# A paged-attention decode step: value pages on every fourth partition, groups of four pages from four blocks, page sums over two groups

## What is computed

```python
# DEC_BATCH 8, DEC_SEQ 4, PAST_LEN 2048, PAGE_SIZE 128, N_HEADS 8, HEAD_DIM 64, MOBA_BLOCK 256, MOBA_TOPK 3
k_full = cache_k[layer, page_table[:, :n_full * ppb]]            # 16 pages a sequence, 2 pages a block
k_mean = jnp.mean(k_full.reshape(db, n_full, ppb * PAGE_SIZE, N_HEADS, HEAD_DIM), axis=2)
gate = jnp.einsum('bthd,bnhd->bhtn', q, k_mean)                  # one score a block
_, sel = lax.top_k(gate, n_sel)                                  # the best 3 of 8 blocks
s_sel = jnp.einsum('bthd,bhtkd->bhtk', qf, k_sel) + bias         # scores of the chosen blocks
p = jax.nn.softmax(jnp.concatenate([s_sel, s_loc], axis=-1), axis=-1)
out = jnp.einsum('bhtk,bhtkd->bthd', p[..., :n_k_sel], v_sel) + jnp.einsum('bhtk,bkhd->bthd', p[..., n_k_sel:], v_loc)
```

## Time and profile before

| | us |
|---|---|
| median of 3 runs | 565.19 (561.32 to 569.01) |
| the profiled execution | 564.61 |
| its span | 562.8 |

### The profile page before, as it was taken

The page is one execution under the profiler, slowest core; times in us unless marked ns, Lnnn a source line. Parts: engine busy times, 40 slices in busy tenths (PEclk is TensorE's granted clock), DMA queues, the critical chain, the costliest instruction groups (busy, mean ns, idle before and its releaser), DMA issues.

```text
span 562.8 us, 13854 instructions
## 1 busy us (share of the span) xinstructions
PE 521.1 (93%) x5624; PEld 474.5 (84%) x5624; DVE 305.9 (54%) x710; ACT 179.9 (32%) x389; POOL 121.4 (22%) x108
## 2 busy tenths in 40 slices
PE   8999999999999999999984899799957899999994
PEld 5999999999999999988984789799846799998763
DVE  6623223577755665667642648875412264694524
ACT  6522222243433433544431222221331132233313
POOL 2101211314132123123132143441451100000002
PEclk9999999999999999999998899899988999999998
DMA  8647443686598999994999989999999795351004
GB/s 247 177 151 195 146 128 103 197 221 186 173 261 197 267 273 210 275 270 123 275 237 289 257 211 265 230 262 272 238 255 226 186 259 192 120 190 38 1 9 149
DMA packets 73561, 112.00 MB, mean 199 GB/s; under 512 B 5501, under 2 KB 35338, under 8 KB 73498
## 3 DMA queue, kind: packets, MB, share of 16 engines
q1 hardware_dynamic: 72122, 107.51, 71.8%
q0 software_dynamic: 1232, 3.36, 2.0%
q10 hardware_dynamic: 144, 0.26, 0.1%
HBM read 106.57 MB, written 4.53 MB: 197 GB/s over the span
## 4 chain that ended last, share of the span: by engine, by line
PE 70%; DMA 17%; DVE 6%; SPq 2%; issue 2%; POOL 1%; ACT 1%; POOLq 0%; DVEq 0%; ACTq 0%
PE BK L576 33%; DMA KRAW<-in_cache_k 17%; PE BK L596 9%; PE BK L916 8%; PE BK L731 4%; PE BK L745 4%; PE BK L665 2%; DVE KT L1326 2%; PE BK L793 2%; PE BK L810 2%; PE BK L800 2%; SPq L504 1%; PE BK L846 1%; PE BK L773 1%; DVE XR L1238 1%
## 5 line engine op out<-in xcount | busy, mean ns | idle before, releaser
L576 PE MATMUL BK<-XH,WH 128*128 128x272 f32 x672 | 202.7, 302 | 0.0
L576 PE MATMUL BK<-XH,WL 128*128 128x272 f32 x672 | 194.3, 289 | 0.0
L576 PE MATMUL BK<-XL,WH 128*128 128x272 f32 x672 | 194.3, 289 | 0.0
L1326 DVE STREAM_TRANSPOSE KT<-KRAW 128x512 f32<-128x512 f32 x128 | 88.6, 701 | 90.4 <-DMA KRAW<-in_cache_k 90.1
L576 PEld LDWEIGHTS BK<-XH,WH 128*128 128x128 f32 x672 | 127.6, 190 | 10.9 <-issue 10.2
L576 PEld LDWEIGHTS BK<-XL,WH 128*128 128x128 f32 x672 | 127.5, 190 | 0.0
L576 PEld LDWEIGHTS BK<-XH,WL 128*128 128x128 f32 x672 | 127.2, 189 | 0.0
L1686 POOL TENSOR_TENSOR WL<-WRAW,WH 128x1024 fp32r<-128x1024 f32 x32 | 76.7, 2397 | 217.6 <-ACT WH L965 217.6
L731 PE MATMUL BK<-KT,QW 128*32 128x128 f32 x1024 | 37.2, 289 | 26.5 <-DVE KT L1326 26.5
L965 ACT ACTIVATE WH<-WRAW 128x1024 fp32r<-128x1024 f32 x52 | 54.9, 1056 | 16.6 <-PE BK L596 16.0
L731 PEld LDWEIGHTS BK<-KT,QW 128*32 128x32 f32 x1024 | 27.7, 115 | 32.4 <-DVE KT L1326 28.9
(11 more groups left out here) (207 smaller groups left out, 807.1 us busy)
## 6 DMA issues: line engine op xcount, KB each, us to landing
KRAW<-in_cache_k SPq DMA_DIRECT2D x128, 256.0 KB, 6.4
WRAW<-in_w_in SPq DMA_DIRECT2D x21, 1024.0 KB, 8.6
VRAW<-in_cache_v SPq DMA_DIRECT2D x56, 256.0 KB, 5.5
VQT<-in_cache_v SPq DMA_DIRECT2D x28, 256.0 KB, 6.3
VEX<-in_cache_v SPq DMA_DIRECT2D x24, 256.0 KB, 7.9
VGU<-in_cache_v SPq DMA_DIRECT2D x20, 256.0 KB, 5.4
WO<-in_w_o SPq DMA_DIRECT2D x4, 1024.0 KB, 7.0
XR<-in_x_prompt SPq DMA_DIRECT2D x4, 512.0 KB, 5.6
```

Source lines behind the costliest of these rows:

```text
L576: last = mm(BK[h][:, 0:HALF], w[:, n % 2, k, :], x[:, k, cols], start=(i == 0 and w is WH and x is XA), stop=(i == KC - 1 and w is WL))
L1326: dve.transpose(KT[:, i % KB, :], KRAW[:, i % KR, :]).then_inc(kt_ok, 1)
```

## The change

Three things, which go together. (1) Group q no longer has pages 4q to 4q+3 but every second page from `first_of(q)`: one page of each of four blocks; two groups make four blocks. (2) `KT` holds a group as piece, t, page j: DVE writes with a step of four elements, PE reads 128 adjacent columns, and column 4t+j belongs to page j. So the turned probabilities of page j lie on partitions j, j+4, ..., and its values are loaded there: `VP[place][j:P:4]`, with the same source, the same four runs of 2 KB in each of 32 partitions. (3) Sums and maxima are taken once for two groups, over 256 columns read with a step of four elements. The adding of the mask (`SC`) walks its columns in the new order. Lines of the changed file stand six to seven further down.

```diff
+def first_of(q):
+
+    return 8 * (q // 2) + q % 2
@@
-        KT = sb("KT", [P, KB, DA])
+        KT = sb("KT", [P, KB // 4, 16, 32, 4])
@@ load_k
-                    sp.load(k_regs, PTB[0:1, i:i + 4])
+                    sp.load(k_regs, PTB[0:1, first_of(i // 4):first_of(i // 4) + 7:2])
@@ load_v
-                sp.load(v_regs, PTB[0:1, 4 * q:4 * q + 4])
+                sp.load(v_regs, PTB[0:1, first_of(q):first_of(q) + 7:2])
@@
-                    sp.dma_start(VP[place][32 * j:32 * j + 32], cache_v[0, bass.ds(page, 1)].rearrange("a (b t) h d -> (a t) b (h d)", b=4)
+                    sp.dma_start(VP[place][j:P:4], cache_v[0, bass.ds(page, 1)].rearrange("a (b t) h d -> (a t) b (h d)", b=4)
@@ page_scores
-                        last = mm(SCB[b % 2][32 * c:32 * c + 32, x * P:(x + 1) * P], QW[:, f, :], KT[:, at4:at4 + 4, 32 * f:32 * f + 32],
+                        last = mm(SCB[b % 2][32 * c:32 * c + 32, x * P:(x + 1) * P], QW[:, f, :], KT[:, q % 2, f].rearrange("p t j -> p (t j)"),
@@ page_turn
-                dve.transpose(KT[:, i % KB, :], KRAW[:, i % KR, :]).then_inc(kt_ok, 1)
+                dve.transpose(KT[:, i // 4 % 2, :, :, i % 4], KRAW[:, i % KR, :].rearrange("p (f d) -> p f d", f=16)).then_inc(kt_ok, 1)
@@ page_sums
-                b, x = q // 4, q % 4
+                b, x = q // 4, q % 4 // 2
@@
-                sc = SCB[b % 2][:, x * P:(x + 1) * P].rearrange("p (n k) -> p n k", n=2)
-                summed = dve.tensor_reduce(R[:, 2 * x:2 * x + 2], sc, AX.X, ALU.add)
-                if x == 3:
+                sc = SCB[b % 2][:, 2 * x * P:(2 * x + 2) * P].rearrange("p (k n) -> p n k", n=4)
+                summed = dve.tensor_reduce(R[:, 4 * x:4 * x + 4], sc, AX.X, ALU.add)
+                if x == 1:
                     link(summed)
-                    last_page = SCB[b % 2][:, 4 * P - 32:4 * P]
+                    last_page = SCB[b % 2][:, 3 * P + 3:4 * P:4]
@@
-                peak = dve.tensor_reduce(KP[:, 2 * x:2 * x + 2], sc, AX.X, ALU.max)
+                peak = dve.tensor_reduce(KP[:, 4 * x:4 * x + 4], sc, AX.X, ALU.max)
@@ choose
-                dve.tensor_tensor(SC[:].rearrange("p (n k) -> p n k", n=8), SCB[b % 2][:].rearrange("p (n k) -> p n k", n=8),
-                                  bass.AP(sel.tensor, sel.offset, [list(sel.ap[0]), [1, 8], [0, 64]]), ALU.add).then_inc(eb_ok, 1)
+                dve.tensor_tensor(SC[:].rearrange("p (x k n) -> p x k n", x=2, n=4), SCB[b % 2][:].rearrange("p (x k n) -> p x k n", x=2, n=4),
+                                  bass.AP(sel.tensor, sel.offset, [list(sel.ap[0]), [4, 2], [0, 64], [1, 4]]), ALU.add).then_inc(eb_ok, 1)
@@ DVE program
-                if t % 4 == 1 and 5 <= t < PAGES:
+                if t % 8 == 1 and 9 <= t < PAGES:
                     page_sums(t // 4 - 1)
```

More of the change, by code:

```diff
@@ L726, in page_scores @@
                     wait(pe, pt_ok, b - 1)
-                at4 = 4 * (q % 2)
                 for k in range(4):
```

## The result

| | before | after |
|---|---|---|
| median of 20 runs on the same chip, us | 568.29 (559.22 to 577.25) | 557.02 (551.14 to 562.13) |
| ratio | | 0.9855 [0.9822, 0.9889] |
| the profiled execution, us (its span) | 564.61 (562.8) | 553.3 (551.5) |

Forecast were 28 us; 557.02 lies 1 us outside the range of 526 to 556. The first view to read is the table of engines on the page of after, with two other lines of that page: the DMA queue of SP, and the shares of the chain of work that ended last.

What follows compares the result with a forecast made beforehand. DMA was taken to bound 273 to 448 us, slowed by value pages, and PE 100 to 262 us. From the profiled 564.6 us, 29.9 less DMA time plus 2 for waits gave 537 us, range 526 to 556.

Steps and rivals of the forecast that it cites:

- 29.9 less and 2 back: DMA, 273 to 448 us: 68 value pages at 351 instead of 221 GB/s save 29.9 us; 2 us added for waits.
- the shape of the load: Value loads: low rate comes from 32 rows of four 2 KB runs, not where they land; time 565 us; chance 0.14.
- I take the write of the same step: nothing: DVE's 128 turnings: writing with a 16-byte step adds 0.03 us a page, 4 us in all, counted as nothing.
- The other bound: DVE's turnings: upper bound from a read with 128-byte step, 1.0 ns an element, 0.5 us a page, 64 us.
- a rival of 0.08: DVE becomes the bound at the turnings; gain shrinks from 0.84 us more each, within 307 us; example 625 us; chance 0.08.
- What hides it: DVE's idle time, 87 us from 273 to 448 us and 56 from 100 to 262, covers the longer turnings.
- two signs of being wrong on DVE: Profile after the change, DVE: turnings exceed 1 us and DVE's share passes 80%.
- turnings 0.5 us longer: DVE's turnings: DVE at 264 of 307 us, prompt attention waits, 5 to 15 us of gain lost; 542 to 552 us; chance 0.06.
- Residual waits: PE, 273 to 448 us: single groups wait for key pages behind value groups and weights; 2 us added.
- SP: counted as nothing: SP's issuing: same rows; page numbers read with a step of two remain one load, hidden behind waits; no cost.
- Reductions, mask and PE: DVE reductions 17.2 to 13.2 us (up to 21.4), hidden; mask counted as nothing; PE's scores stay at 273 ns.
- PE alone as the bound: Whole kernel: all other traffic speeds up too, stalls and low clock go; 528 us; chance 0.17.

Runs made afterwards that it cites:

- e7: Kernel before with only the values moved, each page to every second partition of one half (0 to 63 or 64 to 127); 567.22 us, ratio 0.9978.
- e1: Kernel before with only the value pages moved to every fourth partition, reordered when the mask is added in four pieces; 541.18 us, ratio 0.953.
- e3: Changed kernel with turnings writing 512 adjacent elements, keys of a group then in wrong order; 544.15 us, ratio 0.9577.
- e4: Changed kernel with turnings writing every second element (8-byte step), keys of a group in wrong order; 548.17 us, ratio 0.9594.
- e2: Changed kernel with value pages back on 32 neighbouring partitions, mask added in two pieces that restore page order; 577.41 us, ratio 1.0111.

## Why the prediction was wrong

**DMA: right.** Value pages spread over all partitions move at the pace of weight loads when both share the queue (356 to 408 GB/s, the slices shown under e7), and by e1 this is worth 4.7%. In the stretch that DMA bound, e1 needs 160.9 instead of 186.4 us, 25.5 less; the forecast was 29.9 less and 2 back. That the shape of the load was the cause (a rival with 0.14) is refuted by e1, whose loads have the same shape.

**DVE: the step that failed.** It is the sentence "I take the write of the same step: nothing", which left the longer turnings out of the sum. They measured 0.417 us a page, 49 us of DVE time, and some 16 us of the kernel's time (after against e3). The sentence rested on the copy at L1270, 32 elements in 176 ns with a step of 16 bytes, beside 174 ns for another copy of 32. That is nearly all fixed cost. At 0.81 ns an element 32 elements would be 26 ns, and the copy does not show even that; why not is open. The other bound, 0.5 us a page from the strided reading at L1315, was near the measured 0.417 us, and the third line of evidence was a rule of the Trainium skill on lines, which I had made a rival of 0.08. The Trainium skill (SBUF — State Buffer, section "Specifications (TRN2)") says that SBUF has 16-byte lines, that two hits in a line are needed for full bandwidth, and that each cross to a new line pays. The runs agree: two fp32 in a line are free (e4: 702 against 701 ns), one costs 0.81 to 0.88 ns an element (after; e1 beside e7). My reading of it, a turning several times as long, gave too high a price: the fixed part and the reading stay, and 701 ns become 1118.

**What hides it: half wrong.** I set 87 us of DVE's idle time against the turnings' growth. It hid more than half of it, 16 us lost for 49 us of work. But idle time is an average. The last page of a group is turned behind whatever DVE does for the prompt, and each turning also releases the ring place that the next key load waits for: SP waits 102.3 us for turned keys in after and 88.6 in e3. How much each of these ways cost was not measured apart. The chain of after shows a turning right behind such work, and one that ends just as PE's scores begin after 3.11 us of waiting (chain first, then PE's timeline):

```profile
352.33 2.31 DVE VN L1483
354.65 1.02 DVE KT L1332
...
362.95 1.00 DVE KT L1332
...
364.00 1.08 PE L737 MATMUL BK<-KT,QW 128*32 128x128 f32 x32 [3.11 <-DVE KT L1332]
```

The work ahead of the turning, `VN` at L1483, is itself drawn out, as it is in before (2.60 us): its row in DVE's timeline takes 2.39 us, where others take 0.75, and runs beside a piece of POOL's weight work (`WL`, 351.71 to 354.10 us). In after the same befell the rows that multiply `TG` and `G` (L1358). Here is the first of them, from the timelines of DVE and POOL:

```profile
246.45 2.61 DVE L1358 SCALAR_TENSOR_TENSOR G<-TG,G 128x544 f32<-128x544 f32 x1
...
246.10 2.37 POOL L1692 TENSOR_TENSOR WL<-WRAW,WH 128x1024 fp32r<-128x1024 f32 x1 [8.44 <-ACT WH L971]
```

Seven of these eight rows start while POOL makes a `WL` piece and end some 0.6 us after it; six of them take 2.1 to 2.9 us. In before two do, one of them with 2.48 us, and the rows clear of POOL's work take 0.7. Together the eight grew from 7.6 to 17.5 us. E2, with slow turnings too, has 15.8 us and e3 has 8.7, so the longer turnings had shifted DVE's other work against POOL's, a cost that the forecast had not thought of. What it is worth in the kernel's time was not measured apart.

Where PE had no gap, 4.5 us were lost between the first scores and group 15. The forecast had said that 0 to 262 us would keep its length. Of its two signs of being wrong on DVE one came, turnings over 1 us; DVE's share stayed under 80% (126.52 of 162 us, then 118.30). The rival "turnings 0.5 us longer" (0.06; 542 to 552 us, in terms of a profiled execution) had the mechanism and the size; 553.3 is 1 us above it. In the rival that made DVE the bound, the 307 us leave out 262 to 273 us, whose DVE work is counted; with them DVE has 318 us, and turnings could grow by 0.92 instead of 0.84 us.

**Residual waits: too small.** Two us were added for single groups that wait; e1, whose turnings take 698 ns, still waits 11.1 us for `KT` in all. The next point may be one reason; that was not measured apart.

**SP: counted as nothing, wrong.** The issue of a value page takes twice as long once its partitions are stepped. The rows give min, median and max ns from 100 to 450 us (e7's over the whole execution), first of before, then of after, e2 and e7, with the key pages of after last:

```profile
L504 SPq DMA_DIRECT2D VRAW<-in_cache_v x52: 316/318/1128, 156.3 to 429.7; - x52
...
L511 SPq DMA_DIRECT2D VRAW<-in_cache_v x52: 602/603/1452, 162.7 to 423.5; - x52
...
L511 SPq DMA_DIRECT2D VRAW<-in_cache_v x52: 316/329/1247, 165.0 to 440.2; - x52
...
L504 SPq DMA_DIRECT2D VRAW<-in_cache_v x56: 596/597/1222, 47.4 to 428.2; - x56
...
L491 SPq DMA_DIRECT2D KRAW<-in_cache_k x124: 331/338/1732, 106.6 to 426.6; - x124
```

Eight value issues took 3.9 us from the first to the last before. In the chain of after they take 6.5 us, and the first key page behind them is issued 7.5 us after the first value page instead of 4.4; the key page that the chain goes on with is a later one:

```profile
271.88 0.62 SPq L511
272.69 0.60 SPq L511
273.49 0.60 SPq L511
...
278.33 0.86 SPq L511
279.38 0.44 SPq L491
...
281.03 7.72 DMA KRAW<-in_cache_k
```

With 0.79 us from one value page to the next (272.69, 273.49, 274.28) SP offers an estimated 332 GB/s at most. So value pages alone don't fill DMA: from 293 to 297 us, with four value pages issued from 293.23 us on, the rate is 222 GB/s as before, but at a share of 0.71. The rates over 300 GB/s that the forecast wanted to see come in the windows shown where weights and key pages stand in the queue too.

```profile
293.00:297.00 4.00, 4.00 (x34) 4.00 (x33) 4.00 (x8) 1.51 (x3) 0.00 (x0) 1.00 0.71 222
```

This is also in e1, which still gained 4.7%; what it costs there was not measured apart from the rest.

**Reductions, mask and PE: right.** Reductions take 16 x (383 + 425) ns = 12.9 us, forecast 13.2; the mask 682 ns, as before. One run instead of four in the scores' moving operand: still a median of 273 ns. The granted clock after 273 us rose from 0.94 to 0.97, not to 1.00; in e1 it did rise to 1.00, where no stall for `KT` was longer than 2.6 us (8.0 in before, 3.8 in after).

**PE alone as the bound (528 us, 0.17)** was not reached by any kernel; the best, e1, has PE busy for 160.30 of 173 us from 262 us on.

## What to carry to other kernels

Split a layout change by who pays: which engine writes with a step, which reads with one, and which transfers land where; here the DMA half alone gives 4.7% and the compute half takes some 3 points back, and the permutation fits better into a small operation that is done eight times (the mask) than into one done 128 times. Don't price a strided access by a tiny instruction: take the nearest row with hundreds of elements, even if it is a read or on another tile. And idle time covers an added cost only if the instruction isn't the last link to a waiting engine, doesn't free the buffer that the next load waits for, and doesn't push the engine's other work under another engine's.

## What the runs showed that I had not expected

- SP takes 602 ns instead of 318 to issue a 256 KB load whose partitions are stepped, with a step of four or of two alike (596 ns in e7).
- DVE writes fp32 with a step of 8 bytes at full pace (702 ns for a turning) and pays 0.81 to 0.88 ns an element at 16 bytes; its reading of PSUM with a step of 16 bytes costs nothing (425 ns against 417).
- PE pays for a moving operand in steps of 2048 bytes: 412 against 273 ns for 128 columns, and 2.27 instead of 1.08 us for 32 products. Whether a step of 8 bytes would be free there was not tried.
- A transfer to 32 partitions runs at 233 GB/s within one half of the range, even spread over 64 partitions; on every fourth of all 128 it shares queues that run at 356 to 408.
- A DVE row that multiplies `TG` and `G` (128x544) takes 0.7 us by itself; where it starts while POOL makes a `WL` piece it ends some 0.6 us after that piece, at worst after 2.91 us (seven of eight rows at L1358 in after).
